# Order of the sigmoid and the transposes' high part on ScalarE in a stick-breaking attention stage

## The reference

```
z = q k^T / 8                        (scores of query t and key s)
A[t, s] = sigmoid(z[t, s]) * product over s < j < t of (1 - sigmoid(z[t, j])),   s < t, else 0
out = A v
```

## Time and profile before

| | |
|---|---|
| median of three runs | 1645.64 us (1644.66 to 1656.27) |
| the profiled execution, whole | 1647.07 us |
| its span in the profile | 1645.3 us |
| stick-breaking stage in it | about 494 to 1152 us |
| PE / PEld / DVE / ACT / POOL busy | 98 / 84 / 69 / 44 / 24 % of the span |

### The profile page before, as it was taken

How to read it: one execution, slowest core, us unless ns; L and a number is a source line. 1 busy time by engine, 2 the same in 40 slices (tenths; PEclk the granted TensorE clock), 3 DMA queues, 4 the chain that set the end, 5 groups by cost and what they waited for, 6 DMA issues and landing times.

```text
span 1645.3 us, 26773 instructions
## 1 busy us (share of the span) xinstructions
PE 1605.1 (98%) x9102; PEld 1374.7 (84%) x9102; DVE 1131.1 (69%) x2188; ACT 721.9 (44%) x1788; POOL 399.0 (24%) x236
## 2 busy tenths in 40 slices
PE   5999999999999999999999999999999999999997
PEld 4777888888888888888888888887999999987886
DVE  5731124322227888888888889888678787878888
ACT  5541123201214555555555555555676767641000
POOL 2200000000000111111111111112577778761232
PEclk9999999999999999999999999999999999999999
DMA  5434667555659565955585549532667777465442
GB/s 182 151 119 116 225 222 242 199 157 164 220 201 276 172 186 160 270 164 176 164 266 162 178 146 244 163 124 80 188 146 215 185 201 200 139 201 183 163 157 77
DMA packets 183054, 295.57 MB, mean 180 GB/s; under 512 B 51801, under 2 KB 108500, under 8 KB 178132
## 3 DMA queue, kind: packets, MB, share of 16 engines
q1 hardware_dynamic: 180756, 294.01, 58.1%
q10 hardware_dynamic: 2080, 0.01, 0.1%
q0 software_dynamic: 96, 0.04, 0.0%
HBM read 185.66 MB, written 104.01 MB: 176 GB/s over the span
## 4 chain that ended last, share of the span: by engine, by line
PE 86%; DVE 6%; issue 3%; ACT 1%; DMA 1%; POOL 1%; SPq 1%; DVEq 0%; ACTq 0%; POOLq 0%
PE proj L385 25%; PE proj_a L1074 14%; PE out_ps L1900 7%; PE wt_ps L1043 7%; PE oa_ps L1463 7%; PE pt_ps L1444 4%; PE o_ps L1059 4%; PE o_ps L1057 4%; PE z_ps L1033 3%; PE z_ps L1032 3%; PE s_ps L1435 3%; PE s_ps L1436 3%; DVE WT_lo L1162 1%; DMA b_col<-in_ln_b 1%; PE vtp L407 1%
## 5 line engine op out<-in xcount | busy, mean ns | idle before, releaser
L1107 ACT ACTIVATE WT_hi<-wt_ps 128x512 fp32r<-128x512 f32 (+1 forms) x320 | 171.2, 535 | 297.9 <-PE wt_ps L1043 297.5
L1154 DVE TENSOR_TENSOR_SCAN W<-w,W,zeros 128x512 f32<-128x512 f32 x192 | 257.2, 1340 | 44.0 <-ACT w L1099 42.3
L385 PE MATMUL proj<-h_hi,w_hi 128*128 128x512 f32 x608 | 243.8, 401 | 4.9 <-DVE h_lo L565 3.7
L385 PE MATMUL proj<-h_hi,w_lo 128*128 128x512 f32 x608 | 238.0, 391 | 0.0
L385 PE MATMUL proj<-h_lo,w_hi 128*128 128x512 f32 x608 | 237.4, 390 | 0.0
L1497 ACT ACTIVATE prob<-neg_s,rows 128x256 f32<-128x256 f32 (+1 forms) x384 | 173.6, 453 | 88.6 <-DVE rows L1544 88.0
L1162 DVE TENSOR_TENSOR WT_lo<-wt_ps,WT_hi 128x512 fp32r<-128x512 f32 (+1 forms) x320 | 186.9, 584 | 2.2 <-ACT WT_hi L1107 2.2
L1043 PE MATMUL wt_ps<-ident,W 128*128 128x128 f32 x1088 | 174.0, 275 | 6.8 <-DVE WT_lo L1162 5.5
L1099 ACT ACTIVATE w<-z_ps 128x512 f32<-128x512 f32 (+2 forms) x320 | 169.2, 529 | 8.1 <-PE z_ps L1033 8.1
L1011 POOL TENSOR_TENSOR y_sum<-y_sum,ends 64x512 f32<-64x512 f32 x32 | 34.2, 1070 | 562.8 <-DVE y_sum L1169 562.8
L1043 PEld LDWEIGHTS wt_ps<-ident,W 128*128 128x128 f32 x1088 | 130.4, 140 | 46.0 <-DVE WT_lo L1162 19.2
(11 more groups left out here) (196 smaller groups left out, 3152.8 us busy)
## 6 DMA issues: line engine op xcount, KB each, us to landing
wa_hi<-wa_d SPq DMA_DIRECT2D x48, 512.0 KB, 4.0
wa_lo<-wa_d SPq DMA_DIRECT2D x48, 512.0 KB, 5.1
wa_d<-x_sb SPq DMA_DIRECT2D x24, 512.0 KB, 3.7
va_d<-st SPq DMA_DIRECT2D x48, 256.0 KB, 2.6
va<-va_d SPq DMA_DIRECT2D x12, 1024.0 KB, 8.4
w_raw<-in_w_tiles SPq DMA_DIRECT2D x18, 512.0 KB, 5.1
x_sb<-in_x SPq DMA_DIRECT2D x16, 512.0 KB, 5.5
qk_hi_d<-st SPq DMA_DIRECT2D x32, 256.0 KB, 2.6
```

The source lines that it names most:

```text
L385: last = pe.matmul(acc_of(n)[:], w[w_slot(t)][:, k, :], h[ch][:, k, :], start=(k, a) == (0, 0), stop=(k, a) == (KD - 1, 2))
L1107: act.activation(WT_hi[n % PART_SLOTS][:, cols], t_ps[n % T_SLOTS][:, cols], ACT.Copy) \
L1154: dve.tensor_tensor_scan(W[n % W_SLOTS][:, 0:width][:, ::-1], w[n % W_IN][:, 0:width][:, ::-1], above[:, ::-1], first, ALU.mult, ALU.max). ...
```

## The change

In each step of ACT's loop of the stick-breaking stage the two calls change places: `survive(s)`, the sigmoid of the step's scores, is issued ahead of `high_part(s - 8)`. Nothing is added or taken away, and the waits, buffers and the other engines' programs are the same.

```diff
             act.wait_ge(front.h_stored, front.h_count)
             for s in range(STEPS + VALUES_LAG + 2):
+                if s < STEPS:
+                    survive(s)
                 if 0 <= s - HIGH_LAG < STEPS:
                     high_part(s - HIGH_LAG)
-                if s < STEPS:
-                    survive(s)
                 for a in range(A_GROUPS):
                     if A_END[a] == s - 1:
                         first(a)
```

## The result

The changed kernel takes 1636.37 us (median of 22 runs, 1634.38 to 1648.2) against 1646.02 us before (median of 22 runs taken beside them, 1642.84 to 1656.27). The ratio is 0.9938 with a 95% interval of 0.9925 to 0.9951: 9.7 us, 0.6% faster, inside 1% as forecast and 2.7 us more than the 7.0 of the forecast. The profiled execution took 1635.98 us with a span of 1634.2 us.

The account below looks back on a forecast made before the run. PE, busy 98% of the span, was taken to bound the kernel, stopping only for DVE's low part. Removable stops of 10.0 us less 1.3 and 1.7 gave 7.0 us: 1645.64 - 7.0 = 1638.6 us, range 1633 to 1647 (8 in 10).

Parts of the forecast that it names:

- The bound: Stick-breaking stage: PE sets the pace and stops only before transposes for DVE's low part, 19.2 and 5.5 us recorded.
- The lead: ACT's sigmoid, and DVE's scan behind it, start 0.93 us earlier in full steps, 0.28 with one transpose; 0.6 taken.
- A lead, not a rate: DVE still waits for each sigmoid, only from an earlier position, so its 78.1 us of waits are not the gain.
- The high part later, at no cost: ACT's high part starts 0.15 to 0.5 us later, covered by DVE's scan; low part's 2.2 us wait might double.
- The sigmoid's second wait: On ACT, the sigmoid's wait for the scan four steps back can't bind; no cost.
- The sum: PE's stops in the stage: 10.0 us removable, less 1.3 and 1.7 that stay, gives 7.0 us saved.
- stops that can be taken away: 38 of PE's 42 weight-load stops, before the last score: 19.2 - 1.6 - 38 x 0.2 = 10.0 us.
- the two long ones: Two PE stops of 0.95 us behind one-transpose steps, where the lead is 0.28; 1.3 us stay.
- the conversion: Each PE weight-load stop really loses 0.2 us less than its recorded idle time.
- Nothing changes: Rival: DVE has too much work for some 10 us behind group ends; 0 to 3 us gain, chance 0.21.
- More than forecast: Rival: one PE stop prepares the next; all 10 us plus half of 14.7 set aside go, 17 us; chance 0.10.
- slower: Rival: first scans behind 31 group ends meet POOL, DVE stands 1.11 us each; +15 us, 1660; chance 0.07.

Follow-up runs that it names:

- e2_elsewhere: Kernel before, with the sigmoid ahead of the high part only in the 172 steps outside the five from each group's copy_low on; 1646.93 us, ratio 0.9998.
- low-first kernel: Kernel before with DVE's low part moved ahead of the scan of the same step, ACT's order unchanged; 1632.38 us, run again 1632.57 us.
- e4_small_pool_after: Changed kernel with POOL's two operations at a group's end on 32 of 512 columns, ends and gate left out on the rest; 1632.74 us, ratio 0.9924.
- e5_low_first: First run of the kernel before with DVE's low part ahead of the scan of the same step, ACT's order unchanged; 1632.38 us, ratio 0.9912.

## Why the prediction was right, point by point

**The bound.** PE's stops for the low part were the only place where ACT's order could pay, and the gain lies there. With the traces laid over each other step by step (the difference in time of the same weight load of L1057), 9.5 of the 9.8 us appear in the steps at which the trace of before has a recorded stop.

**The lead.** 0.93 us in a full step and 0.28 with one transpose were forecast and measured. At the two stops of 0.95 us I expected 0.28 to go; 0.35 went.

**A lead, not a rate.** Right: e2_elsewhere has the lead in 172 steps and its weight loads still stop 38 times with 18.2 us. It brought 1.4 us, where the gain shared out by steps would be 5. I added that DVE's wait for the sigmoid would stay near 78 us, and it fell to 66.2. That is no speed-up of DVE either. DVE's busy time stayed (571.6 and 572.3 us in the two windows) while the window lost 9.8 us, so its idle time has to be less by about that; the forecast had left this out.

**The high part later, at no cost.** Right: the low part's wait for it rose from 2.2 to 4.6 us, on DVE's time.

**The sigmoid's second wait.** Right: it doesn't bind. The trace puts six waits of the changed kernel's sigmoid, 3.4 us, down to the scan, but the scan four steps back had ended at least 1.9 us before each sigmoid began.

**The sum.** 7.0 us forecast, 9.8 in the stage. The mechanism was right; the size of one term was not. The low-first kernel has no stop left before the last score, so laid over the kernel before it measures what can be taken away:

| term | forecast, us | measured, us |
|---|---|---|
| stops that can be taken away | 10.0 | 12.9 |
| of these the changed kernel keeps: the two long ones | 1.3 | 1.2 |
| and the others | 1.7 | 2.2 |
| gain in the steps with a stop | 7.0 | 9.5 |

The first term was 2.9 us short, for two reasons. Three of the 13 matmul waits that I had left out as doubles (at 514.56, 733.56 and 815.19 us) have no recorded stop of the weight loads for the low part beside them; they gave 0.4 to 0.5 us each, 1.3 together. And the conversion, 0.2 us less than recorded, was read from steps with full-width scores. In seven stops on the diagonal (573.32, 654.11, 735.24, 816.87, 898.95, 980.63 and 1061.52), where the score matmuls have 256 columns, the step gained what was recorded, 0.34 us for 0.33 at the first for example: 1.5 us more together than I had booked. Why the conversion differs there is not shown. What the changed kernel keeps was nearly right, 3.4 us against 3.0. By my conversion its nine stops before the last score (3.8 us recorded) would be worth only 2.0, which is too little for the same two reasons. So the forecast came out low by a size it had not secured, and inside its range all the same.

**The rivals.** "Nothing changes" had its premise nearly right: in the cluster of the earlier trace rows DVE idles once, the 0.29 us ahead of the scan at 566.55, and then has no recorded break until 574.2 us, past the next two stops. Its conclusion was wrong: the lead taken there is still there at those stops, whose steps became 0.71 and 0.34 us shorter. "More than forecast" asked for 17 us, the 10.0 and half of the 14.7 set aside. The set-aside part did hold lost time, but 2.9 us of it. Whether its loop (a stop delays the next sigmoid) adds something of its own was not separated. For "slower", the scan did go ahead of POOL as I had feared. Timeline of DVE and POOL of the changed kernel behind a group's end:

```profile
883.34 1.27 DVE L1154 TENSOR_TENSOR_SCAN W<-w,W,zeros 128x512 f32<-128x512 f32 x1
...
885.48 2.41 DVE L1154 TENSOR_TENSOR_SCAN W<-w,W,zeros 128x512 f32<-128x512 f32 x1 [0.29 <-ACT w L1099]
...
883.56 1.88 POOL L1011 TENSOR_TENSOR y_sum<-y_sum,ends 64x512 f32<-64x512 f32 x1 [21.81 <-DVE y_sum L1169]
885.51 1.29 POOL L1014 TENSOR_TENSOR y_sum<-y_sum,gate 64x512 f32<-64x512 f32 x1
```

The first scan runs unhindered and POOL's addition, of 1.03 us where nothing meets it, stretches to 1.88 us; then the scan at 885.48 stands for 1.13 us while the multiplication keeps its 1.29. The two rows start 0.03 us apart, the scan's first, so their starts don't tell which of them goes first. This is the pattern of the earlier trace rows. It fits the rule of the Trainium skill, SBUF — State Buffer, on the two sides of SBUF, that such a pair of operations exclude each other for a whole instruction. But it didn't decide: over the stage the mean of the 192 scans is 1343 ns against 1340. Scans of about 2.4 us became more (6 against 1) and those of 1.5 to 2.2 us fewer (7 against 21); those of 384 columns went from 1019 to 1130 ns and those of 256 from 909 to 862. All scans of the stage together took 373.7 us against 371.3.

## What to carry to other kernels

Before an in-order queue is reordered, look for what the bottleneck engine waits for last, and for the deadline of each output: here the transposed block's low part was wanted within two steps and the scan only later, so the low part deserved the first place on its engine, which no total of waits would have told. Time won by starting earlier is a lead: it is worth the stops that it covers, once per backlog, and no more. Where a queue's head waits for a producer while the next entry is ready, as the high part did for the transposes, look at the reader of the one that would be delayed: here the low part stood behind the scan anyway, and the swap cost PE nothing.

## What the runs showed that I had not expected

The granted clock of the matmul engine fell to its lower level (1.2 of 2.4 GHz) behind the stick-breaking stage, where PE had just idled in the short chain of the last eleven steps, and for how long varied from execution to execution. In two profiles, e4_small_pool_after and e5_low_first, it didn't fall there at all, although PE idled there in the same way (five stops with 2.1 us in e5_low_first). Windows 1150 to 1200 us (length, busy PE, PEld, DVE, ACT, POOL, then the clock), e2_elsewhere:

```profile
1150.00:1200.00 50.00, 48.62 (x304) 47.35 (x302) 27.68 (x119) 27.96 (x104) 23.31 (x8) 0.73 0.55 154
```

The same window of e5_low_first:

```profile
1150.00:1200.00 50.00, 50.00 (x416) 49.77 (x415) 36.04 (x158) 33.58 (x129) 26.40 (x9) 1.00 0.81 204
```

A mean of 0.73 is 27 of 50 us at half clock. The program behind the stage then took 497.7 us in e2_elsewhere, 489.6 in e5_low_first at full clock, and 492.9 in the profile of before (clock 0.97 in this window). That is a scatter of 8 us by itself, nearly the size of the effect studied, and why the stage lengths above separate the kernels better than single whole times do. What sets its length in a given execution was not tried.
